# A Hymba-style encoder layer on one core: the front of the recurrence in another order, and three of attention's four square chunks made and summed by GpSimd during attention

## The reference

```python
proj = rms_norm(x, norm_mix_pre) @ w_in        # q, k, v, z, xbc, dt
attn = neighbourhood_attention(q, k, v, rpb)   # 8 heads of 64: 512 channels
attn = rms_norm(attn, attn_out_norm)           # mean of squares over those 512
ssd = ssd_mixer(z, xbc, dt, ...)               # 16 heads, state 128, both directions
mix = concatenate([attn, ssd]) @ w_out
x = x + rms_norm(mix, norm_mix_post)           # then a gated MLP with a conv
```

## Time and profile before

| what | us |
|---|---|
| median of 3 runs | 2894.7 (2892.27 to 2896.05) |
| the profiled execution | 2891.83 |
| its span, first to last instruction | 2890.1 |
| attention of the first sequence, first to last scores | 222.1 to 486.0 |
| front of the first sequence, to the pick of chunk 1's second half | 493.8 to 554.0 |
| rest of the recurrence, first sequence | 554.0 to 639 |

### The profile page before, as it was taken

One profiled execution on the slowest core, in us unless ns is written; L12 is line 12 of the kernel. 1 busy time (PEld: TensorE's weight loads), 2 busy tenths in 40 slices (PEclk: granted clock), 3 DMA queues, 4 the chain that ended last, 5 costly groups with the idle time before them and its releaser, 6 DMA issues.

```text
span 2890.1 us, 36492 instructions
## 1 busy us (share of the span) xinstructions
PE 2788.5 (96%) x12752; PEld 2211.6 (77%) x12752; DVE 2007.6 (69%) x3125; ACT 1284.4 (44%) x2557; POOL 592.9 (21%) x845
## 2 busy tenths in 40 slices
PE   7999999899999999999999999998999999999997
PEld 5778787568777778888778787875677788888875
DVE  3657755784789987775647577458767777778656
ACT  4324555355643333345543255553666333333444
POOL 4622222560014430000100322226500000000001
PEclk9999999999999999999999999998999999999999
DMA  7551232314545541243532412332335222114243
GB/s 226 142 149 54 68 101 90 112 54 160 172 149 179 188 143 59 76 165 117 194 105 71 131 60 75 118 106 70 113 126 191 71 88 81 59 59 160 92 134 129
DMA packets 151253, 334.83 MB, mean 116 GB/s; under 512 B 22353, under 2 KB 25073, under 8 KB 151072
## 3 DMA queue, kind: packets, MB, share of 16 engines
q1 hardware_dynamic: 114864, 206.73, 22.6%
q0 software_dynamic: 36208, 125.77, 13.2%
HBM read 264.51 MB, written 69.90 MB: 116 GB/s over the span
## 4 chain that ended last, share of the span: by engine, by line
PE 77%; DVE 12%; ACT 4%; issue 4%; DMA 2%; POOL 1%; SPq 0%; DVEq 0%; ACTq 0%; POOLq 0%
PE A L1121 5%; PE A L1122 4%; PE A L1123 4%; PE G L1121 4%; PE G L1122 4%; PE G L1123 4%; PE G L668 4%; PE A L1173 4%; PE A L1175 4%; PE A L1174 4%; PE G L669 4%; PE G L670 4%; PE G L698 3%; PE G L699 3%; PE G L700 3%
## 5 line engine op out<-in xcount | busy, mean ns | idle before, releaser
L1765 DVE TENSOR_TENSOR wlo<-raw,whi 128x512 fp32r<-128x512 f32 x626 | 440.7, 710 | 472.7 <-ACT whi L1246 471.1
L1246 ACT CAST whi<-raw 128x512 fp32r<-128x512 f32 x630 | 383.1, 619 | 444.2 <-PE A L1175 147.3
L668 PE MATMUL G<-arena_rounded,whi 128*128 128x512 f32 x768 | 317.9, 414 | 6.7 <-DVE wlo L1765 3.9
L670 PE MATMUL G<-arena_rounded,wlo 128*128 128x512 f32 x768 | 303.7, 395 | 0.0
L669 PE MATMUL G<-arena_rounded,whi 128*128 128x512 f32 x768 | 303.5, 395 | 0.0
L1121 PE MATMUL A<-arena_rounded,whi 128*128 128x512 f32 x560 | 221.8, 396 | 0.5 <-DVE wlo L1765 0.4
L1121 PE MATMUL G<-arena_rounded,whi 128*128 128x512 f32 x560 | 222.0, 396 | 0.3
L1122 PE MATMUL A<-arena_rounded,whi 128*128 128x512 f32 x560 | 221.5, 395 | 0.0
L1123 PE MATMUL A<-arena_rounded,wlo 128*128 128x512 f32 x560 | 221.5, 395 | 0.0
L1123 PE MATMUL G<-arena_rounded,wlo 128*128 128x512 f32 x560 | 221.5, 395 | 0.0
L1122 PE MATMUL G<-arena_rounded,whi 128*128 128x512 f32 x560 | 221.5, 395 | 0.0
(11 more groups left out here) (363 smaller groups left out, 6168.4 us busy)
## 6 DMA issues: line engine op xcount, KB each, us to landing
raw<-w_gu_tiles SPq DMA_DIRECT2D x184, 256.0 KB, 3.4
raw<-w_out_rows SPq DMA_DIRECT2D x144, 256.0 KB, 2.9
raw<-w_tok_tiles SPq DMA_DIRECT2D x96, 256.0 KB, 2.7
raw<-w_in_tiles SPq DMA_DIRECT2D x92, 256.0 KB, 2.8
raw<-sums_of_down SPq DMA_DIRECT2D x88, 256.0 KB, 2.6
raw<-w_down_rows SPq DMA_DIRECT2D x66, 256.0 KB, 3.2
f_by_chunk<-small POOLq DMA_DIRECT2D x24, 512.0 KB, 4.6
arena<-w_down_rows POOLq DMA_DIRECT2D x22, 512.0 KB, 6.5
```

The lines of the kernel that those rows point to most:

```text
L668: nc.tensor.matmul(out, whi[:, u % SPLIT_SLOTS, w], hi, start=first, stop=False)
L670: return nc.tensor.matmul(out, wlo[:, u % SPLIT_SLOTS, w], hi, start=False, stop=last)
L1246: nc.scalar.copy(whi[:, u % SPLIT_SLOTS, w], weights_of(u)).then_inc(S["hi_split"], 1)
L1765: tt(wlo[:, u % SPLIT_SLOTS, w], weights_of(u), whi[:, u % SPLIT_SLOTS, w].bitcast(F), ALU.subtract).then_inc(S["lo_split"], 1)
```

## The change

GpSimd squares the results of attention's pairs 0, 1 and 2 in halves of 512 columns, in the units 20 and 21, 36 and 37, 52 and 53, into key chunks that are no longer needed, adds the second to the first in the units 38 and 39, and adds the third, 1024 columns at once, after the last scores; the sum lies in SF. ACT squares the fourth pair only. `sums` is called twice (at n = 6 and 7) in place of four times. PE runs `back_state(6)` ahead of both `spread`s. The exponents of chunk 0 go to p0 and p1 like all others, and wait until `back_sum(6)` has read those banks; `incoming(0)` goes to p2. DVE runs `back_sum(6)` right after `back_sum(5)`; the eight scalings of `att_scaled` are dealt out between the picks and masses of chunk 0, and the three units of `split_to` come last. A few semaphores are merged (`y_read`, `scratch`), with the same order. The diff, without those renames:

```diff
         def att_square(k):
-            return t(k) if k < 2 else arena[:, (SF, SB)[k - 2], :]
+            return (arena[:, SF, :], t(0))[k]
         def ef_pair(c):
-            return p0 if c else p2
+            return p0
         def eb_pair(c):
-            return p1 if c else p3
+            return p1
                 def sums(k):
-                    pe.wait_ge(S["sq_done"], nth("sq_done", k + 1))
+                    if k:
+                        pe.wait_ge(S["sq_done"], nth("sq_done", 1))
+                    else:
+                        pe.wait_ge(S["sum_ready"], nth("sum_ready", 1))
...
                 def exponents(c, g):
...
                             elif c == 0:
-                                pe.wait_ge(S["cb_out"], nth("cb_out", 1))
-                                pe.wait_ge(S["xv_out"], nth("xv_out", TT))
+                                pe.wait_ge(S["b_read"], nth("b_read", 7))
+                            elif c == 1:
+                                pe.wait_ge(S["picked"], nth("picked", 2))
                             else:
                                 pe.wait_ge(S["yib_out"], nth("yib_out", c))
                         else:
                             if g:
                                 pe.wait_ge(S["m_ready"], nth("m_ready", 2 * c + 1))
-                            elif c == 0:
-                                pe.wait_ge(S["xa_out"], nth("xa_out", 2 * TT))
-                                pe.wait_ge(S["am_full"], nth("am_full", 8))
-                            elif c > 1:
+                            elif c:
                                 pe.wait_ge(S["m_ready"], nth("m_ready", 2 * c))
...
                     if g == 0:            # within
                         if c:
                             pe.wait_ge(S["u_ready"], nth("u_ready", c))
                         else:
-                            pe.wait_ge(S["ef_exp"], nth("ef_exp", 2))
+                            pe.wait_ge(S["yib_out"], nth("yib_out", 1))
...
                     if n % 2:             # PE, the front
                         back_state(n // 2)
-                    if n >= 5:
-                        sums(n - 5)
+                    if n >= 6:
+                        sums(n - 6)
                 back_state(4)
-                sums(3)
                 pe.wait_ge(S["xa_out"], nth("xa_out", 2 * TT - 1))
                 inner(0, A[:, 0, :])
                 back_state(5)
+                back_state(6)
                 spread(0)
                 spread(1)
-                back_state(6)
                 exponents(0, 0)
-                pe.wait_ge(S["b_read"], nth("b_read", 7))
-                incoming(0, SB, p0, "yib_done")
+                pe.wait_ge(S["xa_out"], nth("xa_out", 2 * TT))
+                pe.wait_ge(S["xv_out"], nth("xv_out", TT))
+                pe.wait_ge(S["cb_out"], nth("cb_out", 1))
+                incoming(0, SB, p2, "yib_done")
                 exponents(0, 1)
...
                         else:             # c == 0, ahead of inner(1)
-                            pe.wait_ge(S["m_ready"], nth("m_ready", 2))
+                            pe.wait_ge(S["am_full"], nth("am_full", 8))
...
                     nc.scalar.copy(...xtok...)        # ACT, loop over n
+                    if n == 4:
+                        act.wait_ge(S["sum_ready"], nth("sum_ready", 1))
                     nc.scalar.copy(...B...)
-                    if n > 2 and n < 7:
-                        square(n - 3)
+                    if n == 3:
+                        square_last()
...
                 back_sum(4)               # DVE, end of the front
                 roots(-1)
                 back_sum(5)
-                att_scaled(0)
-                att_scaled(1)
                 back_sum(6)
-                split_to(UNITS_TO[J_OUT] + 3)
+                att_scaled(0, (0, 1))
                 pick(0, 0)
+                att_scaled(0, (2,))
                 from_behind(0)
                 masses(0, 0)
+                att_scaled(0, (3,))
+                att_scaled(1, (0,))
                 pick(0, 1)
+                att_scaled(1, (1, 2))
                 masses(0, 1)
+                att_scaled(1, (3,))
+                split_to(UNITS_TO[J_OUT] + 3)
...
                     m.then_inc(S["q_ready"], 1)       # POOL, unit st
+                    for first, pair_at, to in ((20, 0, K), (36, 1, K + 1), (52, 2, K + 2)):
+                        if st in (first, first + 1):
+                            cs = slice((st - first) * HALF, (st - first + 1) * HALF)
+                            pool.wait_ge(S["q_ready"], nth("q_ready", st + 1))
+                            if st == first:
+                                pool.wait_ge(S["o_out"], nth("o_out", 16 * (pair_at + 1)))
+                            nc.gpsimd.tensor_tensor(arena[:, to, cs], arena[:, Q + pair_at, cs], arena[:, Q + pair_at, cs], ALU.mult
+                                                    ).then_inc(S["pool_step"], 1)
+                            pool.wait_ge(S["pool_step"], step())
+                    if st in (38, 39):
+                        ...
+                        nc.gpsimd.tensor_tensor(arena[:, K, cs], arena[:, K, cs], arena[:, K + 1, cs], ALU.add).then_inc(S["pool_step"], 1)
+                        pool.wait_ge(S["pool_step"], step())
...
+                pool.wait_ge(S["s_done"], nth("s_done", UNITS))
+                pool.wait_ge(S["q_ready"], nth("q_ready", UNITS))
+                nc.gpsimd.tensor_tensor(arena[:, SF, :], arena[:, K, :], arena[:, K + 2, :], ALU.add).then_inc(S["sum_ready"], 1)
...
                     pool.wait_ge(S["xv_out"], nth("xv_out", i + 1))   # POOL, by_head
+                    if i == 1:
+                        pool.wait_ge(S["sum_ready"], nth("sum_ready", 1))
```

## The result

| | kernel before | changed kernel |
|---|---|---|
| median, us (six runs each) | 2894.56 | 2878.68 |
| lowest to highest, us | 2890.94 to 2897.64 | 2877.54 to 2881.93 |
| ratio, 95% interval | | 0.9947 (0.9935 to 0.9960) |
| profiled execution, us (its span) | 2891.83 (2890.1) | 2877.54 (2875.8) |

The change is faster by 15.9 us between the medians and by 14.3 us between the profiled executions. The prediction was 2882 with a range from 2873 to 2890.

A forecast was written before the change was run, and what follows sets the result against it. PE is nearly always busy except in the fronts, where no engine is full, so time is won there: 15.1 us from two fronts less 3.1 in attention is 12.0, giving 2882 us, range 2873 to 2890.

The forecast's parts named there:

- main case: Whole kernel: fronts win 15.1 us, GpSimd's work in attention costs 3.1, giving 2882 us; chance 0.5.
- The walk through the front: Front from 507.74 to chunk 1's second pick, instruction by instruction: that pick at 546.75 against 554.01, 7.3 us earlier.
- GpSimd's hold in `back_sum(6)`: Front: GpSimd's weighting for the forward state starts 0.2 us ahead of DVE's scaling and costs it 1.7 us.
- The splits: Front: three weight splits behind chunk 0's last scaling take 2.85 us, leaving DVE free at 541.0.
- chunk 1's exponents: Front: they wait for the second masses (537.5), end at 538.4, hidden by the splits; without that cover also no cost.
- Two sets of sums are 3.4 of each 7.3: Front: dropped sums give 3.4 us of each 7.3 us gain; moved scalings and splits give the rest.
- Attention: GpSimd's squares and sums hold DVE: 0.8 us in unit 20, 0.65 in unit 36, 0.1 at the end; 1.55 per sequence.
- Half clock: Rival, front: PE pauses bring the 1.2 GHz clock, costing 1.75 us per sequence, 2886 us; chance 0.2.
- the argument from DVE's list: Front, against the half-clock rival: DVE's list covers a slow PE until `within(0, 1)`, which would end at 546.85.
- The other argument: Front, against the half-clock rival: none of PE's pauses in the new order is 3 us.
- a late `within` in the loop: Loop over chunks: sign of being wrong, `within` or POOL's `add` late so that the front's gain is given back.
- POOL gives way: Rival: no DVE hold in attention and none in `back_sum(6)`; gain 18.5 us, 2876 us; chance 0.12.

The follow-up runs named there:

- e3: Changed kernel, with GpSimd's weighting of x for the forward state waiting for the last back_sum instead of the last back_state; 0.9934 of the kernel before.
- e8: Changed kernel with the three weight splits again ahead of the first pick, behind the last back_sum; 0.9948 of the kernel before.
- e4: Changed kernel with GpSimd's squares and additions in attention moved to units 42 to 54, away from convolution steps; 0.9946 of the kernel before.
- e6: Changed kernel with one GpSimd square of 1024 columns at units 20 and 36 in place of two of 512; 0.9966 of the kernel before.
- e7: Changed kernel with the eight scalings of attention's result together again ahead of the last back_sum; 0.9972 of the kernel before.
- e2: Changed kernel's new front order, but four ACT squares, four sets of sums and no GpSimd squares or additions in attention; 0.9943 of the kernel before.
- e5: Changed kernel with GpSimd's forward-state weighting waiting for the last back_sum, and its attention squares and additions at units 42 to 54; 0.9926 of the kernel before.

## Why the prediction came out as it did

The forecast of 12.0 us against the profiled execution was 2.3 us short of the measured 14.3, and its main case is the one that happened. But one duration in it was wrong, and so was the way in which it divided the gain between the sums and the order. That the whole time followed the four parts so closely is luck: the 1.4 us lost at the end of the recurrence, which the prediction did not have, were made up by the output projections.

- **The walk through the front** held. Shifted by 1.4 us for attention's loss, it put the first pick at 529.7 and the second at 535.25; they came at 529.77 and 535.15. GpSimd's hold in `back_sum(6)` was put at 1.7 and measured at 1.59 (e3).
- **The splits** were the one duration I took from a row that did not fit the new place. 2.85 was their time beside GpSimd's product, which in the kernel before ran from 532.47 to 534.37; in the new place nothing held them, and they took 1.89. From there on the walk was 1.2 us late: I had chunk 1's picks at 541.0 and 546.75, 542.4 and 548.1 with the shift, and they came at 541.19 and 546.89. That is the 2.3 us that were missing, about half of it in each sequence. The prediction also said that chunk 1's exponents would cost nothing without the splits as cover; its own numbers had them end 0.25 us behind the last scaling, and in e8 DVE waited 0.79 and 0.68 for them, at the lower clock.
- **"Two sets of sums are 3.4 of each 7.3"** was wrong. They are PE's 3.4, but from 520 on the chain is on DVE. The sums bring 2.2 in the old order and 1.1 in the new one, since by ending earlier they bring GpSimd's weighting onto DVE's scaling. What I put to the sums belongs to the order: 7.4 in the first front where my sum left it 3.9. The walk hid this: it had the hold in it, but I priced the halves by PE's time, and not by walking each alone.
- **Attention** came out at 1.51 and 1.62 for my 1.55, partly by luck. The hits at the units 20 and 36 were there (0.57 and 0.53 for my 0.8 and 0.65), and one that I had excluded came in: GpSimd's addition held a split (0.69 to 1.60), which put off the softmax of the next two units. In unit 40 PE transposes the second of them directly behind the scores, with no projection between, so that the lateness has nowhere to go. I had looked for convolution steps, and not for such units.
- **Half clock.** The clock did fall to 0.50 in the changed kernel, at 536 to 540, but DVE's scalings and splits ran on until 541, and PE was back at 1.00 for `within(0, 1)` (1.90 in 542.75). It cost nothing there: the slow exponents of chunk 1 ended at 540.09 and DVE was free at 541.19, as the argument from DVE's list said. The other argument, that none of the pauses is 3 us long, failed: behind pauses of 2.78 the clock fell in four of eight cases. Where it costs is ahead of the first exponents, which I had not thought of (e4 and e6 paid 1.3 to 2.5 us for it), and at the end of the recurrence, where the changed kernel paid 0.72 and 0.65. The prediction had named a late `within` in the loop as a sign of being wrong; in this small measure it came.
- **POOL gives way** gave 2876 and is as near to the measured time as the forecast, with a mechanism that e3 and e6 rule out. My reading of the Trainium skill needs a correction here: I used "Advanced Engine Details and Errata", VectorE Performance Modes, alone. The same page's GPSIMD Details, and "GPSIMD Engine Reference", Key points, name two cases in which DVE and GpSimd contend: the two-port modes, and DVE instructions with two inputs from SBUF. The runs agree with the second one: the scalings (2.82 for 1.22), the convolution steps (3.17 and 4.02 for 2.60) and the splits (1.60 for 0.69) have two such inputs, and the additions with one operand from PSUM kept 1.22 beside GpSimd's work. How long such a hold is, e6 shows: it grows one for one with GpSimd's instruction.

What stays open: why the clock falls behind one pause of 2.78 us and not behind another of the same length, and why it fell at the end of the recurrence in some kernels and not in others; and the few us by which the rest of the program differs between executions, which make the whole time a blunt measure of the smaller edits.

## What to carry to other kernels

Price the halves of a change each by its own walk in the order in which it will stand: work dropped from an engine is worth its time only while that engine is the one the chain is on, and here 3.4 us less on TensorE were worth 1.1, because VectorE had become the bound and GpSimd came to stand in its way. When GpSimd gets elementwise work, look at what VectorE does at that moment, and put it where VectorE has slack or reads from PSUM: one changed wait and other units for the same instructions gave another 5.65 us by the parts. A duration may be taken from a row only if what ran beside it there will run beside it again.

## What the hardware showed that I had not expected

GpSimd's product of a tile with itself is cheaper than that of two tiles: 1.04 for 512 columns and 1.89 for 1024, where two different tiles take 1.28 (a product) and 2.36 (an addition). And an operation of DVE with a single tile as input can be held as well: the last unit's scaling by one number per row, 0.32 us in the kernel before, took 1.02 beside GpSimd's last sum (487.52 to 489.90). Before and after:

```profile
487.62 0.32 DVE L1992 TENSOR_SCALAR small<-small,rinv 128x192 f32<-128x192 f32 x1
...
489.01 1.02 DVE L1996 TENSOR_SCALAR small<-small,rinv 128x192 f32<-128x192 f32 x1
```

A pause of TensorE is not told from its length alone. Ahead of the first exponents the changed kernel, e4, e6 and e8 paused 2.77 to 2.78 us in each of their two sequences: behind four of these eight pauses the four exponents took 1.16 to 1.17, and behind the other four 1.60 to 2.05. Behind the two pauses of 7.04 in e7 they took 2.04 and 2.05. Behind the six pauses of 0.49 to 1.18 in e2, e3 and e5 they took 1.16 to 1.17 every time.
